# Norm factors applied behind the products with rows turned in the producing phase, and gate columns placed in small groups in the recurrences

## The reference

```python
def rmsnorm(x, g):
    return x * lax.rsqrt(mean(x * x, axis=-1) + 1e-6) * g
def swiglu_ffn(x, g, w_gate, w_up, w_down):
    h = rmsnorm(x, g)
    return (silu(h @ w_gate) * (h @ w_up)) @ w_down
def first_block(x, ...):
    for i in range(2):
        x = x + 0.5 * swiglu_ffn(x, ffn1_norm[i], ...)
        h = rmsnorm(x, mix_norm[i])
        x = x + (even_mixer if i % 2 == 0 else odd_mixer)(h, ...)
        x = x + 0.5 * swiglu_ffn(x, ffn2_norm[i], ...)
    return rmsnorm(x, final_norm)
```

## Time and profile before

| | |
|---|---|
| median of 3 runs | 3329.39 us (3326.44 to 3334.41) |
| the profiled execution | 3335.18 us, of which the span (first to last instruction) is 3333.3 us |
| mean granted clock of PE | 0.976 of 2.4 GHz |
| gate columns in the chains | the first of layer 0 at 1350.7 us of the span, the last of layer 1 at 2177.7 us |

### The profile page before, as it was taken

The page is one execution under the profiler, slowest core; times in us unless marked ns, Lnnn a source line. Parts: engine busy times, 40 slices in busy tenths (PEclk is TensorE's granted clock), DMA queues, the critical chain, the costliest instruction groups (busy, mean ns, idle before and its releaser), DMA issues. The chain is left out here.

```text
span 3333.3 us, 48125 instructions
## 1 busy us (share of the span) xinstructions
PE 3227.9 (97%) x20197; PEld 1905.6 (57%) x20197; DVE 1368.7 (41%) x2542; ACT 561.6 (17%) x1281; POOL 170.0 (5%) x157
## 2 busy tenths in 40 slices
PE   8999999999999989899999899899999999999999
PEld 7845686784568567676685576774433333333333
DVE  7643475764456534614564346332221211111122
ACT  1113310110221033213111223130200000000000
POOL 0001000000000002301001104010100000000000
PEclk9999999999999999879999999799999999999999
DMA  7442045344324440114444421033599999899993
GB/s 287 187 150 102 29 174 202 117 174 178 127 83 172 157 172 26 64 55 155 174 168 173 160 77 63 10 151 142 209 391 393 402 393 396 351 396 391 398 398 143
DMA packets 81046, 665.61 MB, mean 200 GB/s; under 512 B 10529, under 2 KB 11169, under 8 KB 14017
## 3 DMA queue, kind: packets, MB, share of 16 engines
q1 hardware_dynamic: 76320, 651.27, 50.1%
q10 hardware_dynamic: 4512, 11.27, 0.9%
HBM read 661.45 MB, written 1.05 MB: 199 GB/s over the span
## 5 line engine op out<-in xcount | busy, mean ns | idle before, releaser
L3952 PE MATMUL psum<-ring,arena 128*32 128x512 f32 x5376 | 587.8, 593 | 0.0
L756 PE MATMUL psum<-ring,arena 128*128 128x256 f32 x1760 | 406.6, 379 | 1.7 <-DVE arena L919 1.7
L3952 PEld LDWEIGHTS psum<-ring,arena 128*32 128x32 f32 x5376 | 172.8, 110 | 389.0 <-issue 388.1
L756 PEld LDWEIGHTS psum<-ring,arena 128*128 128x128 f32 x1760 | 330.1, 190 | 46.3 <-DVE arena L919 3.7
L756 PE MATMUL psum<-ring,xT_norm 128*128 128x256 f32 x1320 | 304.7, 381 | 0.3
L3984 PE MATMUL psum<-ring,arena 128*32 128x512 f32 x2688 | 293.6, 592 | 0.7 <-DVE arena L4116 0.7
L756 PEld LDWEIGHTS psum<-ring,xT_norm 128*128 128x128 f32 x1320 | 251.3, 191 | 35.7 <-issue 1.7
L869 DVE TENSOR_TENSOR ring<-ring 128x1024 f32<-128x1024 f32 x220 | 268.0, 1220 | 1.9
L786 PE MATMUL psum<-ring,arena 128*128 128x512 f32 x440 | 207.4, 592 | 0.0
L4112 DVE TENSOR_TENSOR arena<-arena,psum 128x256 f32<-128x256 f32 x84 | 35.6, 423 | 410.9 <-ACT arena L4086 410.9
L3984 PEld LDWEIGHTS psum<-ring,arena 128*32 128x32 f32 x2688 | 88.5, 110 | 200.2 <-issue 190.9
(11 more groups left out here) (584 smaller groups left out, 3581.2 us busy)
## 6 DMA issues: line engine op xcount, KB each, us to landing
ring<-in_moe_w SPq DMA_DIRECT2D x340, 1024.0 KB, 7.2
ring<-in_ffn_w SPq DMA_DIRECT2D x50, 2048.0 KB, 7.9
ring<-in_ffn_w SPq DMA_DIRECT2D x65, 1024.0 KB, 4.9
ring<-in_merge_w SPq DMA_DIRECT2D x16, 2048.0 KB, 8.6
ring<-in_feat_w SPq DMA_DIRECT2D x12, 2048.0 KB, 8.9
ring<-in_ev_in_w SPq DMA_DIRECT2D x4, 2048.0 KB, 9.2
ring<-in_od_in_w SPq DMA_DIRECT2D x4, 2048.0 KB, 8.5
ring<-in_merge_w SPq DMA_DIRECT2D x8, 1024.0 KB, 11.8
```

The source lines that it names most:

```text
L756: last = pe.matmul(psum[:, bank, 0:GROUP], a[:, k, :], w[:, k, :], start=(fresh and k == 0), stop=(k == KT // 2 - 1), skip_group_check=True)
L3952: last = pe.matmul(psum[part(j), r, :], xg[:, u.i, u.group // GROUPS, r * P + BLOCK * j:r * P + BLOCK * (j + 1)], m[:, j, :], start=(u.i = ...
```

## The change

Two things. **The norms.** Two classes take the place of `Tail` and `Head` at six boundaries (FFN 0, the even mixer, FFN 1, FFN 2, the odd mixer, and layer 0's join, each to what follows). `Exit`, in the producing phase, turns rows 0 to 127 (`FIRST_ROWS`) as soon as they are added, and ScalarE copies them to xT with the gain. `Entry`, in the consuming phase, turns rows 128 to 255 (`LAST_ROWS`), squares them, and forms `rstd` beside the first products; whoever takes a product of un-normed rows out of PSUM multiplies by `rstd`. `first_norm` goes (FFN 0 has an `Entry` for all four blocks). FFN 3 keeps `Tail`; FFN 4 turns its first rows with an `Exit` without squares, for `embedding.add`. **The chains.** The same 64 gate columns and the same other work, in another order. The core of the diff:

```diff
+class Exit:
+    def on_tensor(self, pe, i):
+        pe.wait_ge(self.added, i + 1)
+        turn_block(self.prog, pe, FIRST_ROWS[i], self.banks[i]).then_inc(self.turned, 1)
+    def on_scalar(self, act):
...
+        for i, (b, n) in enumerate(FIRST_ROWS):
+            if self.norm:
+                act.wait_ge(self.added, i + 1)
+                square_block(prog, act, (b, n), self.junk[:, i, :]).then_inc(self.squared, 1)
+            act.wait_ge(self.turned, i + 1)
+            for k in range(4):
+                m = 4 * n + k
+                act.activation(prog.xT[:, m, b * P:(b + 1) * P], prog.psum[:, self.banks[i], k * P:(k + 1) * P], ACT.Copy,
+                               scale=1.0 if self.gain is None else self.gain[:, m:m + 1]).then_inc(self.copied, 1)
+class Entry:
+    def on_tensor(self, pe):
+        for block, bank in zip(self.blocks, self.banks):
+            turn_block(self.prog, pe, block, bank).then_inc(self.turned, 1)
...
+    def on_vector(self, dve):
...
+            dve.wait_ge(self.turned, i + 1)
...
+                dve.tensor_tensor(to, of, spread(self.gain[:, 4 * n:4 * n + 4].unsqueeze(2), 4, P), ALU.mult).then_inc(self.copied, 1)
+    def on_scalar(self, act):
...
+            square_block(self.prog, act, block, self.junk[:, i % 2, :]).then_inc(self.squared, 1)
+        act.wait_ge(self.mean_ready, 1)
+        act.activation(self.prog.mean, self.prog.mean, ACT.Sqrt).then_inc(self.rooted, 1)
...
-LAST_PRODUCTS = ("P1", "P6", "P5", "P7", "P4", "P3", "P2")
+LAST_PRODUCTS = ("P1", "P2", "P6", "P5", "P3", "P7", "P4")
@@ feed_forward, PE: after the down products of the last two pairs
+                if then != "norm":
+                    if name == "P5":
+                        tail.on_tensor(pe, 0)
+                    elif name == "P7":
+                        pe.wait_ge(p1_copied, total + 1)
+                        tail.on_tensor(pe, 1)
@@ feed_forward, ACT and DVE
-                    act.activation(silu[:, 0, :], first_gate, ACT.Silu).then_inc(silu_ready, 1)
+                    act.wait_ge(entry.ready, 1)
+                    act.activation(silu[:, 0, :], first_gate, ACT.Silu, scale=prog.rstd[:, 0:1]).then_inc(silu_ready, 1)
-                act.activation(silu[:, 1, :], gate1, ACT.Silu).then_inc(silu_ready, 1)
+                act.activation(silu[:, 1, :], gate1, ACT.Silu, scale=prog.rstd[:, 1:2]).then_inc(silu_ready, 1)
-            head.on_vector(dve)
...
-            for i in range(4):
-                mix_x(i)
-                sum_up(0, i)
...
+                sum_up(0, 0)
+                entry.on_vector(dve)
+            dve.wait_ge(entry.copied, len(entry.blocks))
+            mix_x(0)
+            entry.mean_on_vector(dve)
+            sum_up(0, 1)
+            mix_x(1)
+            entry.invert_on_vector(dve)
+            mix_x(2)
+            sum_up(0, 2)
+            sum_up(0, 3)
+            mix_x(3)
-                dve.tensor_tensor(up[:, 1, :], silu[:, 1, :], up[:, 1, :], ALU.mult).then_inc(posted, 1)
+                dve.scalar_tensor_tensor(up[:, 1, :], up[:, 1, :], prog.rstd[:, 1:2], silu[:, 1, :], ALU.mult, ALU.mult).then_inc(posted, 1)
@@ add_projection, PE: products in the order (0,0), (0,1), (1,0), (1,1)
+                    if n >= 2 and k == 3:
+                        tail.on_tensor(pe, n - 2)
@@ join_branches, layer 0, PE: behind products 2 and 3 of that same order
+                    if j and n >= 2 and exit_gain is not None:
+                        if n == 2:
+                            pe.wait_ge(weighted, 12)
+                        tail.on_tensor(pe, n - 2)
@@ both mixers: the products' evacuations, such as
-            dve.tensor_copy(z[:, 1, KPOS:KPOS + 512], proj(2, 1)).then_inc(z_vector, 1)
+            dve.tensor_scalar(z[:, 1, KPOS:KPOS + 512], proj(2, 1), prog.rstd[:, 1:2], None, ALU.mult).then_inc(z_vector, 1)
@@ chains, PE (first_to_32 and second_to_32 call fill(1) ahead of each j in `between`)
             for q in range(4):
                 repeat_row(next(again), 1)
                 turn(q)
-                fill(1)
-            first_to_32(0)
-            fill(2)
+            fill(1)
+            first_to_32(0, (4, 8, 12))
+            fill(1)
+            repeat_row(next(again), 1)
+            second_to_32(0, (2, 5, 8, 11, 14))
+            fill(1)
             repeat_row(next(again), 1)
             fill(1)
-            second_to_32(0)
-            fill(2)
-            repeat_row(next(again), 1)
-            fill(2)
             first_to_64(0)
-            fill(2)
+            fill(1)
             repeat_row(next(again), 1)
             second_to_64(0)
             fill(2)
+            first_to_128(0, 0)
+            first_to_128(0, 1)
             turn(4)
             turn(5)
-            first_to_128(0, 0)
-            first_to_128(0, 1)
+            second_to_128(0, 0)
             turn(6)
-            second_to_128(0, 0)
+            second_to_128(0, 1)
             turn(7)
-            second_to_128(0, 1)
             r_rhs_first()
             g_u(0)
+            first_to_32(1, (8,))
             fill(1)
-            first_to_32(1)
-            fill(2)
             r_u(0, 2)
-            fill(1)
-            second_to_32(1)
-            fill(1)
+            second_to_32(1, (4, 8, 12))
             g_out(0)
```

More of the change, by code:

```diff
@@ L638, with feed_forward @@
 POSTED = {name: i + 1 for i, name in enumerate(("u2", "v", "up1", "gate1", "hidden1", "up0", "hidden0"))}
-def feed_forward(prog, weights, gain, factor=1.0, after=(), side=None, loads=None, meanwhile=None, norm_next=True):
+def feed_forward(prog, weights, gain, factor=1.0, after=(), side=None, loads=None, meanwhile=None, fresh=False, exit_gain=None, then="rows"):
     total, psum, ring = FF_PAIRS, prog.psum, prog.ring
@@ L692, in feed_forward @@
         silu_ready, copied, p1_copied = (ph.semaphore(n) for n in ("silu_ready", "hidden_copied", "p1_copied"))
-        head = Head(prog, ph, xn, gain)
-        tail = Tail(prog, ph, junk, [(1, 1), (1, 0), (0, 1), (0, 0)])
+        entry = Entry(prog, ph, entry_junk, gain, (6, 7, 3, 4), FIRST_ROWS + LAST_ROWS if fresh else LAST_ROWS)
+        if then == "norm":
+            tail = Tail(prog, ph, junk, [(0, 0), (0, 1), (1, 1), (1, 0)])
+        else:
+            tail = Exit(prog, ph, junk, exit_gain, (DOWN_BANK["P2"], DOWN_BANK["P1"]), norm=(then == "rows"))
         for part in (side, meanwhile):
@@ L816, in _ @@
             prog.wait_load(act, "cols")
-            head.on_scalar(act)
+            if fresh:
+                prog.wait_load(act, "x")
+                act.activation(prog.warm, prog.ident[:, 0:1], ACT.Sqrt)
+            entry.on_scalar(act)
             for c in range(total):
@@ L971, in _ @@
             add(0, 0, p1_wide).then_inc(settled, 1)
+            wait_acc("P2")
+            dve.wait_ge(settled, 1)
+            add(0, 0, acc("P2")).then_inc(tail.added, 1)
             wait_acc("P6")
@@ L978, in _ @@
             add(0, 1, u2_wide).then_inc(settled, 1)
+            wait_acc("P3")
+            dve.wait_ge(settled, 5)
+            add(0, 1, acc("P3")).then_inc(tail.added, 1)
             wait_acc("P7")
@@ L986, in _ @@
             add(1, 0, acc("P4"), -factor).then_inc(tail.added, 1)
-            wait_acc("P3")
-            add(0, 1, acc("P3")).then_inc(tail.added, 1)
-            wait_acc("P2")
-            add(0, 0, acc("P2")).then_inc(tail.added, 1)
-            if norm_next:
+            if then == "norm":
                 tail.on_vector(dve)
@@ L1006, in add_projection @@
         copied = [ph.semaphore("copied_by_scalar"), ph.semaphore("copied_by_vector")]
-        tail = Tail(prog, ph, junk, [(b, n) for n in range(2) for b in range(TB)])
+        tail = Exit(prog, ph, junk, gain, (4, 5))
+        columns = FIRST_ROWS + LAST_ROWS
         @ph.block.tensor
@@ L1042, in _ @@
                    .then_inc(copied[1], 1)
-            for i, (b, n) in enumerate(tail.order):
+            for i, (b, n) in enumerate(columns):
                 dve.wait_ge(bank_full, i + 1)
@@ L2144, in first_to_32, with second_to_32 @@
                             last.then_inc(first_32, 1)
-            def second_to_32(c):
+            def second_to_32(c, between=()):
                 for by in range(2):
@@ L2643, in _ @@
             join_64(0)
-            for q in range(4, 8):
+            for q in range(4, 7):
                 expand(q)
             join_128(0, 0)
+            expand(7)
             join_128(0, 1)
@@ L3462, in join_branches @@
     o_bank = lambda n: 2 * (n % 2)
-    columns = [(b, c) for c in range(2) for b in range(TB)]
+    columns = FIRST_ROWS + LAST_ROWS
     adds_before = np.cumsum([0] + [x > 0 for j, x, b in tiles]).tolist()
@@ L4293, in scale_on_pool, with add @@
         pool.wait_ge(self.scaled, 2 * TB)
[L4295 removed]
+    def add(self, weights, gates, junk, last, entered=False):
         prog, e = self.prog, self.e
```

220 lines of the change are left out of this document (129 added, 91 removed).

## The result

The changed kernel takes 3299.57 us as the median of 5 runs (3285.22 to 3306.64), the kernel before 3329.39. The ratio is 0.9901, 95% interval 0.9874 to 0.9928: 30 us faster. The profiled execution took 3306.64 us, its span 3304.8 at a mean clock of 0.981. With the runs made beside the experiments, on other chips, the 11 runs of the changed kernel have a mean of 3300.0, and 52 of the kernel before 3335.3.

A forecast was written before the change was run, and what follows sets the result against it. PE, busy 97% of the span, bounds the kernel; only its idle time and low-clock stretches can save much. Norms -16.1 and chains -27 sum to -43.1 us: 3329.4 to about 3286 us, range 3258 to 3319.

The forecast's parts named there:

- Part A: Norms at six phase boundaries, FFN 3's tail and the start: less idle time and shorter transposes, 16.1 us gained.
- The cover of the factor: Boundary entries: `rstd` ready some 3 us after the barrier, under first P1 and P2 (3.62 us); margin 0.6 us per boundary.
- Part B: Both layers' chains, reordered gate columns: -28.2 us of clock, -4 of issue waits, +5.2 of new waits, -27 us together.
- First stretch: Chains' first stretch at a lowered clock: gone in layer 0 (-3.4 us), half gone in layer 1 (-2.6 us).
- Middle stretch: Chains' middle lowered-clock stretch: gone in both layers (-11.8 and -10.4 us), granted clock 0.9 or more there.
- Last stretch: Chains' last lowered-clock stretch, from g_u to g_out: kept, five columns for five, clock about 0.6.
- Issue waits: L2156 and L2153 in the chains: 4 us of 10.9 us of issue waits go, as columns let issue run ahead.
- New waits: Chains, from moved columns and shorter covers, less the covered wait at turn 4: +2.6 us per layer, 5.2 in all.
- All stretches go: Rival: filling the gaps ahead of each fall also removes the chains' last stretch, 24.9 us more, about 3262 us; chance 0.25.
- The columns don't hold the clock: Rival: columns among small products are too little for the chains' clock, only the norms gain, about 3314 us; chance 0.27.
- The slower rival: Chains' turns lose their clock without their four columns and the level stays down: +14 us, about 3343 us; chance 0.04.
- The rival of a new wait at the boundaries: Late factor or exit turns waiting for their add: up to 3 us at six boundaries, about 3302 us; chance 0.07.

The follow-up runs named there:

- exit turns behind the product: Changed kernel with add_projection's exit turns behind the third and fourth product instead of in their middle: both phases 32.73 us for 32.30; whole 3316.9 us in one run.
- chains only: Norms of the kernel before, chains function of the changed kernel: 3310.62 us median, ratio 0.9914 to the kernel before.
- groups alone: Changed kernel with the old order around the products of 128, gate columns still in the new small groups: 3319.27 us median, ratio 0.9930 to the kernel before.
- norms only: Norms changed, chains function as in the kernel before: 3309.94 us median, ratio 0.9922 to the kernel before.
- order alone: Norms changed, and of the chains only the order around the products of 128, gate columns where they were: 3302.03 us median, ratio 0.9887 to the kernel before.
- a kernel that is 11 us faster on the mean: Changed kernel with a gate column behind each of turns 0 to 3 and five, not three, inside the second second_to_32: medians 3280.62 and 3287.09 us.
- shift of instructions: Changed kernel plus 64 products of zeros ahead of layer 1's first turn: 3291.34 us in one run; with columns back among the turns, 3299.51 us median.

## Why the prediction was right, and where its terms were off

The range held the time (3258 to 3319), the sign was right, and the forecast lay 14 us low: 43 us were forecast, 30 measured, 35 over all chips. One of its signs failed: layer 1's middle stretch, forecast at 0.9 or more, ran at 0.50 in the profile of the changed kernel.

**Part A (16.1 us).** The mechanism and the size hold. Idle time per boundary is 1.12 as taken, transposes 1.06 for 0.97. The phase table gives 18.8 us without the even mixer's attention (2.2 + 1.5 + 2.3 + 6.4 + 3.2 + 0.5 + 1.7 + 1.0), the split of the runs 13.2 without any change of clock. The forecast's 16.1 held a clock term without naming it. It took the old transposes at their measured 16.90 us, of which 3.8 are the lower level (the four longer ones against 2.18 each), and the new ones at full clock. That part came true; without it the forecast is 12.3 for the 13.2.

The cover of the factor was argued on a wrong time. It was taken as ready 3 us after the barrier, under P1 and P2; it comes 5.2 us after it (403.6 - 398.45), 0.6 us after P2's end. It costs nothing all the same, because the Silu would wait 2.59 us longer for VectorE; in the even mixer, too, PE shows no new wait. The small terms: the start gave 0.7 for 0.9 taken (its 2.2 us in the phase table are partly given back in FFN 0). The join's exit cost 0.42 for 0.75, and the experiment with the exit turns behind the product shows that this is its place. FFN 3's tail cost 0.40 as taken (PE's wait for the scaled rows behind it is 8.09 us for 7.69). FFN 4's phase gave 1.0 where nothing was taken; 0.6 of it is a wait of its down products that stands in the kernel before alone:

```profile
PE psum L786 <- DVE arena L880: 0.6, 1, 0.6
```

**Part B (27 us).** By itself it gave 23 us (chains only), behind the norms 11. The term that was off is the one of 28.2 us for the lower level. Its parts:
- *First stretch, gone in layer 0, half gone in layer 1.* In layer 0 it was gone in 10 of the 11 profiles with columns inside second_to_32 (3.4 us in the other), and there in all three without, so these columns work. In layer 1 it was there in all profiles but one, and its length, 7 to 44 us, differs by execution: 37 and 7 for the same kernel. Its mean is 17 us over the 11 profiles with columns and 10.2 us in each of the three without, so it was not halved. Where it was long it ran through the middle stretch. That case wasn't in the forecast.
- *Middle stretch, gone in both.* Right in that no fall begins there any more, and by the reason given, the order around the turns: groups alone left it in layer 0.
- *Last stretch, kept.* Right: 17 to 27 us in both profiles of the changed kernel, until five columns stood inside the second second_to_32.
- *The price.* Half of each us was taken; the runs give 0.42 to 0.43.
- The mean time at 1.2 GHz fell from 133 (norms only) to 106: 27 us x 0.43 = 12 us for the 28 forecast. Without the norms it fell from 159 to 107: 22 us. So the term was near its size alone; the sum of both parts took it as unchanged by the norms, and the runs don't bear that out.
- *Columns or order.* The forecast gave 6 us of the term to the columns and 22 to the order. The order alone took 12 us off the time at 1.2 GHz of norms only, though within the scatter; adding the groups to the order changed the mean time by 2 us, adding them without it by 5 the wrong way, neither clear.

*Issue waits (4 us)*: the profile's sum for L2153, L2156 and L2141, 13.5 us, fell by 9.4. *New waits (5.2 us)*: the turns' four columns cost 2.1 us a layer where 1.7 was taken; the order gave back 4.0 for 3.0 taken. With both signs the rest came to +0.7 us against norms only (3254.4 and 3253.7) for +1.2 forecast.

**The rivals.** "All stretches go" did not happen here; a kernel that is 11 us faster on the mean comes near it, and its last stretch went by more columns inside the same section, as that rival had it. "The columns don't hold the clock" (3314) is out as a time, but near the truth for the groups of this change: order alone did as well. The slower rival is out: no level fell at the first turns, and giving their columns back changed nothing in it; what it named, a fall that stays down over later work, did occur, but from second_to_32 on. The rival of a new wait at the boundaries is out: PE's list shows none there but the barrier. The trace agrees with half of the rule cited from the Trainium skill (TensorE: Matmul & The Clock Gate, "HAM oscillation"): all falls of the chains stand in or behind gaps. A full queue doesn't end them, as 18 us of layer 1 at 0.50 with PE busy throughout show again, and neither do large products (41 us at 0.50 with 17.7 us of 128x512 among them).

Partly open: why layer 1 falls near 60 us of its chains when layer 0, with the same program, doesn't. In the profiles with the new columns, layer 1 has a wait for issue more there than layer 0: 0.84 to 1.12 us in second_to_32, or 2.2 to 2.5 us in first_to_32 in three profiles without columns in that section. The one profile with neither has no fall. What moves these waits wasn't isolated. Open: how long a fall lasts; and the 17 to 24 us in the even mixer's attention, which 5 of 14 profiles showed. The two profiles with the old norms (before and chains only) don't have it, but their runs scatter as widely.

## What to carry to other kernels

Where a matrix engine's clock has two levels, find the waits just ahead of each fall and fill those. Put engines' waits behind work that is already queued: that order alone did as well as order and regrouping together. Large products inside a section of small ones helped where they removed its waits for issue (the last stretch, with five), taken from right beside; they didn't end a fall once it had begun. Look at the next section before taking any from it. Compare such kernels by their time at the lower level and the rest separately: with six runs of each, the rest tells 2 us apart where the times tell 10. And measure each part of a change with and without the other: gains in clock need not add up.

## What the runs showed that was not expected

The kernel before varies by 35 us on one chip (3321 to 3356), and what varies with it is the time at the lower level of TensorE's clock, 133 to 201 us. A single profile told wrong twice: it showed layer 1's chains as 2.7 us slower with the change (the next one 10 us faster), and it made the shift of instructions look like a cure. The norms' change, which moves no product of the chains, took clock falls away too: those at the boundaries.
